# One tile later: weight splits, x tiles and gates of a projection kernel in float16 pairs, and the order of its first loads

## What is computed

```
xn   = rmsnorm(x, norm_gain)
proj = xn @ w_in                       # 1024 x (9*512 + 8)
gb, gc, hc, zc, q, k, v, o, zm, ig, fg = split(proj)
yc, conv_new = short_conv(gc * hc, conv_buf, conv_w)     # 3 taps
y_conv = gb * yc * silu(zc)
# mLSTM, 4 heads of 128, in chunks of 128 tokens, with running maxima
lf = log_sigmoid(fg + b_fgate); igh = ig + b_igate; b = cumsum(lf)
d  = exp(log_d - m_t); s = (q k^T) * d
h  = (s v + inter * q c_prev) / max(|den|, exp(-m_t))
c, n, m = new states, per chunk and per sample
y_m = rmsnorm(h) * mh_norm_gain * sigmoid(o) * silu(zm)
out = [y_conv, y_m] @ w_out ;  y = rmsnorm(x + out, final_norm_gain)
```

## Time and profile before

| what | us |
|---|---|
| median of three runs | 1125.42 (1124.85 to 1126.02) |
| the profiled execution | 1124.19 |
| its span, first to last instruction | 1122.4 |
| TensorE busy with matmuls | 1068.5 |
| vector engine busy | 538.1 |
| scalar engine busy | 340.3 |
| GpSimd busy | 256.6 |
| mean granted TensorE clock, of full speed | 0.987 |

### The profile page before, as it was taken

The page is one execution under the profiler, slowest core; times in us unless marked ns, Lnnn a source line. Parts: engine busy times, 40 slices in busy tenths (PEclk is TensorE's granted clock), DMA queues, the critical chain, the costliest instruction groups (busy, mean ns, idle before and its releaser), DMA issues. The chain is left out here.

```text
span 1122.4 us, 17994 instructions
## 1 busy us (share of the span) xinstructions
PE 1068.5 (95%) x7186; PEld 603.8 (54%) x7186; DVE 538.1 (48%) x1005; ACT 340.3 (30%) x672; POOL 256.6 (23%) x333
## 2 busy tenths in 40 slices
PE   2899999999999999899999997999999999999996
PEld 2555546565666555456665554566656555444442
DVE  4786664566443434574534344744333323333333
ACT  6546434243303242234122322422212221211111
POOL 6102303021201322111122231111111111442422
PEclk9899999999999999899999998999999999999998
DMA  9574532043200311442003115300212053255652
GB/s 223 161 154 88 133 80 48 24 123 99 69 26 12 94 44 57 136 118 69 20 18 90 48 57 147 107 32 19 93 38 90 20 197 114 97 199 203 236 211 81
DMA packets 124183, 108.73 MB, mean 97 GB/s; under 512 B 42384, under 2 KB 109092, under 8 KB 124100
## 3 DMA queue, kind: packets, MB, share of 16 engines
q1 hardware_dynamic: 84160, 66.78, 20.9%
q0 software_dynamic: 7600, 25.03, 6.1%
q10 hardware_dynamic: 32340, 15.78, 5.4%
HBM read 65.43 MB, written 33.41 MB: 88 GB/s over the span
## 5 line engine op out<-in xcount | busy, mean ns | idle before, releaser
L805 PE MATMUL bank<-xTh,Wh 128*128 128x512 f16 (+2 forms) x1304 | 422.7, 343 | 6.5 <-DMA xTl<-to 3.5
L806 PE MATMUL bank<-xTl,Wh 128*128 128x512 f16 (+2 forms) x1304 | 425.5, 343 | 0.0
L807 PE MATMUL bank<-xTh,Wl 128*128 128x512 f16 (+2 forms) x1304 | 424.8, 343 | 0.0
L807 PEld LDWEIGHTS bank<-xTh,Wl 128*128 128x128 f16 x1304 | 129.4, 99 | 121.7 <-issue 3.1
L805 PEld LDWEIGHTS bank<-xTh,Wh 128*128 128x128 f16 x1304 | 129.4, 99 | 115.7 <-DMA xTl<-to 3.7
L806 PEld LDWEIGHTS bank<-xTl,Wh 128*128 128x128 f16 x1304 | 129.4, 99 | 109.9 <-issue 4.2
L814 PE MATMUL bank<-Wh,xTh 128*128 128x128 f16 x544 | 92.8, 219 | 0.6 <-DVE ysum L163 0.6
L816 PE MATMUL bank<-Wh,xTl 128*128 128x128 f16 x544 | 92.8, 219 | 0.0
L815 PE MATMUL bank<-Wl,xTh 128*128 128x128 f16 x544 | 92.8, 219 | 0.0
L163 ACT ACTIVATE tz<-bank 128x512 f32<-128x512 f32 x32 | 19.1, 598 | 147.9 <-PE bank L807 147.1
L677 POOL TENSOR_TENSOR ysumst<-ysum,ysumst 128x1024 f16<-128x1024 f32 x16 | 34.8, 2178 | 106.5 <-ACT ysumst L163 106.5
(11 more groups left out here) (336 smaller groups left out, 1520.9 us busy)
## 6 DMA issues: line engine op xcount, KB each, us to landing
wst<-in_w_in ACTq DMA_DIRECT2D x27, 512.0 KB, 4.0
xs<-in_x_prompt SPq DMA_DIRECT2D x22, 512.0 KB, 4.1
y_ops<-ysumst POOLq DMA_DIRECT2D x16, 512.0 KB, 3.2
w_ops<-xs SPq DMA_DIRECT2D x16, 448.0 KB, 3.8
out<-xs POOLq DMA_DIRECT2D x11, 512.0 KB, 2.9
Wh<-y_ops SPq DMA_DIRECT2D x12, 448.0 KB, 3.6
Wl<-y_ops SPq DMA_DIRECT2D x12, 448.0 KB, 4.3
wst<-in_w_in SPq DMA_DIRECT2D x9, 512.0 KB, 4.6
```

Of the source, the lines that this page charges most:

```text
L805: mm(out, wh[:, k, :], xh, start=(k == 0), stop=False)
L806: mm(out, wh[:, k, :], xl, start=False, stop=False)
L807: last = mm(out, wl[:, k, :], xh, start=False, stop=(k == KT - 1))
```

## The change

It changes the tables, the first loads, and the place of the weight splits.

```diff
-X_SQUARE = [{Q: 6, GC: 7, HC: 8, ZC: 9, O: 10}, {K: 11, V: 12, GC: 13, HC: 14}, {K: 15, V: 16}]
-X_PARTS = [{Q: 5, GC: 6, HC: 7, GB: 8, O: 9, ZM: 10}, {V: 11, Q: 12, HC: 13, GB: 14}, {V: 15, Q: 16}]
-GATES_AT = [ZC, GC, GC]
-SCAN_AT = [O, GB, GB]
-TURN_AT = [ZM, ZC, ZC]
+X_SQUARE = [{Q: 6, GC: 7, HC: 8, ZC: 9, O: 10}, {K: 11, Q: 12, HC: 13, GB: 14}, {K: 15, V: 16}]
+X_PARTS = [{Q: 5, GC: 6, HC: 7, GB: 8, ZM: 9}, {V: 10, Q: 11, GC: 12, GB: 13, ZC: 14}, {V: 15, Q: 16}]
+GATES_AT = [ZC, HC, GC]
+SCAN_AT = [O, ZC, GB]
+TURN_AT = [ZM, O, ZC]
...
@@ SP, the start
-            turn_x(0)
-            turn_x(1)
-            load_w(sp, 0, 1)
-            turn_x(2)
-            load_w(sp, 0, 2)
-            turn_x(3)
-            load_rows(sp, states_in, 0, ...)
-            turn_x(4)
+            for unit in range(X_EARLY):
+                turn_x(unit)
...
@@ GpSimd, the start
             x_power(2)
+            x_power(3)
+            x_power(4)
             step(pool.memset(ones[:, :], 1.0))
...
-            x_power(3)
             for tile, first_of, rest, start in (...):
                 step(pool.memset(tile[:, :], rest))
                 step(pool.memset(first_of[:, :, 0], start))
-            x_power(4)
...
@@ TensorE, at_half
                 if t == V and first and b == 0:
+                    pe.wait_ge(states_in, 16 * 2)
+                    use_t1(3)
+                    nc.tensor.transpose(T1[:, 0:STATES_IN], prow[...], ident[...]).then_inc(t1_full, 1)
                     columns(1, MIX, t1(g, b, "mix cols", first))
...
@@ TensorE, first tile
                             if c == CH - 1:
-                                pe.wait_ge(states_in, 16 * 2)
-                                use_t1(2)
-                                nc.tensor.transpose(T1[:, 0:STATES_IN], prow[...], ident[...]).then_inc(t1_full, 1)
-                                gates(x_units(0), MIX, BT, 3)
+                                gates(x_units(0), MIX, BT, 2)
...
@@ scalar engine, act_block
                 if following == "weights":
-                    act.wait_ge(w_low, (g + 1) * NT - 1)
+                    act.wait_ge(w_low, (g + 1) * NT)
                     act.wait_ge(wo_low, 4 * g)
-                    load_w(act, g + 1, 0)
-                    load_w(act, g + 1, 1)
+                    for t in range(STAGES):
+                        load_w(act, g + 1, t)
...
-                    if following == "weights":
-                        act.wait_ge(tile_done, nth(g, b) * NT + (t + 1))
-                        split_w(g + 1, t)
-                        if t < NT - 2:
-                            act.wait_ge(w_low, (g + 1) * NT + t)
-                            load_w(act, g + 1, t + 2)
+                    if following == "weights" and t:
+                        act.wait_ge(tile_done, nth(g, b) * NT + t)
+                        split_w(g + 1, t - 1)
+                        if STAGES <= t + 1 < NT:
+                            act.wait_ge(w_low, (g + 1) * NT + (t - 1))
+                            load_w(act, g + 1, t + 1)
+                    if g and b == 0 and t == K:
+                        act.wait_ge(tile_done, g * NB * NT)
+                        split_w(g, ZM)
...
@@ scalar engine, the start
             x_square(3)
+            load_w(act, 0, 1)
+            x_square(4)
             x_high_part(2)
+            load_w(act, 0, 2)
+            x_high_part(3)
+            load_rows(act, states_in, 0, ...)
             split_w(0, 0)
-            x_square(4)
-            x_high_part(3)
+            x_high_part(4)
             act.wait_ge(bias_in, 16 * 3)
             gate_logits(0, MIX, 1)
-            x_high_part(4)
...
@@ vector engine, dve_block
-                    if following == "weights":
-                        if t == K:
+                    if following == "weights" and t:
+                        if t == V:
                             gain_w(g + 1, K)
-                        if t < NT - 1:
-                            gain_w(g + 1, t + 1)
-                        split_w(g + 1, t)
+                        gain_w(g + 1, t)
+                        split_w(g + 1, t - 1)
+                    if g and b == 0 and t == K:
+                        split_w(g, ZM)
...
@@ vector engine, the start
             x_low_part(2)
+            x_low_part(3)
             split_w(0, 0)
-            x_low_part(3)
-            gain_w(0, 1)
+            x_low_part(4)
             dve.wait_ge(bias_in, 16 * 3)
             gate_abs(0, MIX)
-            x_low_part(4)
+            gain_w(0, 1)
             gain_w(0, 2)
-            dve.wait_ge(t1_full, 3)
-            mark(copy(par[:, 0:STATES_IN], T1[:, 0:STATES_IN]).then_inc(t1_free, 1), t1_free, 3)
...
             split_w(0, 2)
+            dve.wait_ge(t1_full, 4)
+            mark(copy(par[:, 0:STATES_IN], T1[:, 0:STATES_IN]).then_inc(t1_free, 1), t1_free, 4)
             gate_scan(1, MIX, BT)
```

More of the change, by code:

```diff
@@ L470, in _ @@
             load_x(4)
-            turn_x(0)
-            turn_x(1)
-            load_w(sp, 0, 1)
-            turn_x(2)
-            load_w(sp, 0, 2)
-            turn_x(3)
-            load_rows(sp, states_in, 0, state_n.rearrange("b h p -> (b h) p"), state_conv.rearrange("b j (h p) -> (b j h) p", p=P))
-            turn_x(4)
+            for unit in range(X_EARLY):
+                turn_x(unit)
             next_w(3)
@@ L881, in at_half @@
                 if t == V and first and b == 0:
+                    pe.wait_ge(states_in, 16 * 2)
+                    use_t1(3)
+                    nc.tensor.transpose(T1[:, 0:STATES_IN], prow[0:STATES_IN, :], ident[0:STATES_IN, 0:STATES_IN]).then_inc(t1_full, 1)
                     columns(1, MIX, t1(g, b, "mix cols", first))
@@ L985, in pe_block @@
                             if c == CH - 1:
-                                pe.wait_ge(states_in, 16 * 2)
-                                use_t1(2)
-                                nc.tensor.transpose(T1[:, 0:STATES_IN], prow[0:STATES_IN, :], ident[0:STATES_IN, 0:STATES_IN]).then_inc(t1_full, 1)
-                                gates(x_units(0), MIX, BT, 3)
+                                gates(x_units(0), MIX, BT, 2)
                             x_turned(pe, 1 + c)
@@ L1340, in _ @@
             x_square(3)
+            load_w(act, 0, 1)
+            x_square(4)
             x_high_part(2)
+            load_w(act, 0, 2)
+            x_high_part(3)
+            load_rows(act, states_in, 0, state_n.rearrange("b h p -> (b h) p"), state_conv.rearrange("b j (h p) -> (b j h) p", p=P))
             split_w(0, 0)
-            x_square(4)
-            x_high_part(3)
+            x_high_part(4)
             act.wait_ge(bias_in, 16 * 3)
             gate_logits(0, MIX, 1)
-            x_high_part(4)
             mixed_start(0, 0, K, True)
@@ L1351, in _ @@
             split_w(0, 2)
-            gate_logits(1, BT, 3)
+            gate_logits(1, BT, 2)
             gate_logs(1, BT)
@@ L1793, in dve_block @@
                     at_end(g, b, t, first)
-                    if following == "weights":
-                        if t == K:
+                    if following == "weights" and t:
+                        if t == V:
                             gain_w(g + 1, K)
-                        if t < NT - 1:
-                            gain_w(g + 1, t + 1)
-                        split_w(g + 1, t)
+                        gain_w(g + 1, t)
+                        split_w(g + 1, t - 1)
+                    if g and b == 0 and t == K:
+                        split_w(g, ZM)
                     if (g, b) in SLAB_FIRST and t in (GB, ZM):
                         output_low(SLAB_FIRST[g, b] + (t == ZM))
-            GATE_COUNTS = [1, 3] + [t1(0, b, "gates", True) for b in range(NB - 1)]
+            GATE_COUNTS = [1, 2] + [t1(0, b, "gates", True) for b in range(NB - 1)]
             COLS_COUNTS = ([t1(0, 0, "mix cols", True)] + [t1(0, b, "cols", True) for b in range(NB - 1)] +
```

## The result

The changed kernel takes 1116.57 us (median of 4, 1115.34 to 1118.71) where the kernel before, on the same chip, takes 1125.72 (median of 4): ratio 0.9922, 95% interval 0.9904 to 0.9940. That is 9.2 us faster. Forecast were 16.6; the median is 0.07 us above the top of the range. The profiled execution is the slowest of the four, 1118.71 us; against the profiled one of before, 1124.19, it is only 5.5 faster. Further on, one of the five executions of experiment 1 (3989.05 us) and one of the fifteen of before beside it (1412.27) stand far from all others, and the ratios leave them out.

The account below looks back on a forecast made before the run. TensorE was taken as the bound, busy 1068.5 of 1122.4 us, so only its idling could shrink. Terms -16.2, -2.2 and +1.8 gave -16.6 us, from 1125.42 to 1108.8 us; range 1104.0 to 1116.5.

Parts of the forecast that it names:

- part 2: Start: weight and state loads leave SP's list, transposes finish sooner, block 0's gates start sooner; net 2.2 us won.
- part 1: Weight blocks of heads 1 and 2: weight splits one tile later remove `dp` waits and slow clock; 16.2 us won.
- part 3: Block 1 of head 0: x tiles, gates and scan move one tile later; small waits go, T1 waits; 1.8 us lost.
- rival (c): Weight blocks: the load's wait moves; a late third load returns half of 16.2 between GC and ZC: 1116.9; chance 0.11.
- about 0.5 us each, ahead of `kf`'s evacuation, which nobody needs before Q's half: Weight blocks: the scalar engine issues three loads in a row instead of two, about 0.5 us each, without delaying TensorE.
- I take it that this one keeps it: Block 1: the new 3.5 us T1 gap keeps full clock, as a 3.5 us gap at line 805 did.
- Rival (a): Block 1's gap is 4 us or more and costs the clock, 2.6 us: 1111.4; chance 0.14.
- The clock may hold there, but the chain, not TensorE, sets 56.1, so this is worth nothing: Start, behind block 0's gates: the vector engine's chain sets the time, so a held clock wins nothing.
- Rival (b): Start: moved loads slow the transposes as much as before, gaining only 0.9 us: 1110.1; chance 0.13.
- (d): Block 1: GpSimd finishes its sums so early that T1's wait is only 1 us: 1106.3; chance 0.04.
- (e): Block 1: tile 12's late load delays its square, the sums, states and T1: 1128 or more; chance 0.03.
- (f): Weight blocks: neither line 849 wait goes, because something else, such as y sums, holds `dp`: 1125; chance 0.03.

Follow-up runs that it names:

- experiment 1: Kernel before with only the later weight splits and the three weight loads issued together: 1111.88 us, ratio 0.9901.
- experiment 5: Changed kernel with the scalar engine's third weight load issued behind tile K's evacuation and the sample states behind tile V's: 1115.84 us, ratio 0.9926.
- experiment 8: Changed kernel with the edits of experiment 5, experiment 6 and experiment 7 together: 1107.54 us, ratio 0.9858.
- experiment 9: As experiment 8, but the three weight loads stay at the block's head and only the states move to the end of V: 1105.24 us, ratio 0.9836.
- experiment 11: As experiment 8, with unread 128-column products filling three TensorE waits in block 0 of head 0: 1104.31 us, ratio 0.9828.
- experiment 10: As experiment 8, with the final gain's broadcast load moved behind the loads of the third phase's operands: 1105.13 us, ratio 0.9835.
- experiment 13: Mended kernel: changed kernel with the states' place of experiment 9 and the edits of experiment 6, experiment 7, experiment 10 and experiment 11: 1103.71 us, ratio 0.9819.
- experiment 14: Kernel of experiment 13 without part 3, with the tables and GpSimd's list of before: 1106.93 us, ratio 0.9848.
- experiment 15: Kernel of experiment 13 without part 2: the start's order of before, its own waits filled with unread products: 1107.43 us, ratio 0.9854.
- experiment 6: Changed kernel with GpSimd's power of tile 12 behind the four sums of y in block 1: 1112.53 us, ratio 0.9899.
- experiment 7: Changed kernel with block 1's scan moved to tile O and its turn to ZM: 1113.82 us, ratio 0.9914.
- experiment 12: Changed kernel with 58 unread products filling TensorE's wait for T1 in block 1: 1113.92 us, ratio 0.9914.
- experiment 4: Changed kernel without part 3, with the five tables of before: 1111.98 us, ratio 0.9899.
- experiment 2: Kernel before with only the new order at the start: 1123.04 us, ratio 0.9995.
- experiment 3: Kernel before with only the changed tables, moving x tiles, gates and scan of block 1: 1128.38 us, ratio 1.0048.

## Why the prediction was wrong

**The sign was right, and in the profiles the parts' signs too** (part 2 can't be told from nothing by the times), and so were most of the waits, in place and size: gates of block 0 at 28.24 (27 to 28.5 was said), the wait at the half of V 1.76 (1.8), T1's wait 3.34 (3.5), chunk 2's 2.69 (2.2); the waits of `dp`, `ysum` and `cs` gone, the clock full in both weight blocks. What failed is what stood beside the waits. The median lacks 7.4 of the 16.6 us, the profile 10.7: 3.8 in part 1, 2.0 in part 2, 4.7 in part 3. That the median lies beside rival (c)'s 1116.9 is chance, since the wait that (c) names came at a fifth of its price (1.6 of 8.1 us).

**Part 1, 11 to 13 us instead of 16.2.** The failed step is "about 0.5 us each, ahead of `kf`'s evacuation, which nobody needs before Q's half". Both halves of it are wrong. The three loads took 3.04 us to issue (0.41, 0.66 and 1.92) and the states 3.03 and 3.75, where two loads and the states took 1.08 and 1.67 before. And TensorE needs `kf` evacuated some 6 us after K's end, not at Q's half: V's products, from 459.5 to 465.5, fill the other bank, and Q's first one goes into K's, which `kf` still held until 466.79. Two waits, 1.34 and 2.02, are the price, and experiment 5 takes them away by moving the issues and nothing else. The bound of "0 and 1 us a block" for a late vector engine was right for after (0.65 and 0.90 at the chunks), but only because `kf` waited first; without that it is 1.5 to 2.9 in head 2 (experiments 5, 8, 9 and 11), and 0.7 to 1.1 once the gain's load is moved too (10, 13, 14 and 15), a transfer that the prediction hadn't looked at.

**Part 3, 5.4 us lost instead of 1.8.** The failed step is "I take it that this one keeps it": a gap of 3.50 us in the trace of before left the clock alone, so one of 3.5 would. It did not. The step takes a limit from one execution, and that execution speaks against it: the same trace has the clock at 0.50 from 49 to 56, where TensorE had waited 1.39 us (until 47.60) and 1.58 (until 50.26). And where before kept it, at line 805, experiment 1, whose start is the same, lost it behind a shorter wait. Windows of before, then the wait and the window of experiment 1:

```profile
28.00:30.00 2.00, 0.53 (x9) 0.36 (x6) 1.19 (x5) 0.00 (x0) 1.08 (x7) 1.00 0.89 151
50.00:52.00 2.00, 1.74 (x7) 1.16 (x8) 1.76 (x4) 1.69 (x7) 0.00 (x0) 0.50 0.00 0
```

```profile
26.64 0.29 PE L805 MATMUL bank<-xTh,Wh 128*128 128x128 f16 x1 [3.11 <-DMA xTl<-to]
...
28.00:30.00 2.00, 1.56 (x15) 1.35 (x14) 0.29 (x2) 0.00 (x0) 1.06 (x7) 0.50 0.89 155
```

So the 3.50 that kept the clock was luck of that execution. Rival (a), at a chance of 0.14, had the outcome but not its condition, a gap of 4 us or more, and the outcome came twice: 3.1 us of slow clock behind T1's wait and 1.7 behind chunk 2's, which no rival had. The waits themselves add up to what was forecast. By the timeline:

- won before the exponentials: 1.64 (1.3 was said)
- T1's wait: 3.50 lost (3.5)
- gates without a wait: 1.27 won (1.3)
- chunk 1 and 2: 1.91 less 0.77, 1.1 lost (0.9)
- slow clock: 3.1 and 1.7, 4.8 lost (0)

The sum without the last line is 1.7, against the forecast's 1.8. Experiment 6 takes T1's wait away and wins 6.4, the wait and its clock together; the wait for `cn` at chunk 2 stays, 2.70, with its slow clock. Experiment 7 takes chunk 2's and wins 3.5 in the profile; experiment 12 keeps T1's wait and takes only the clock's part, 3.3. The clock's part is that of these profiles: behind the same T1's wait it was 1.7 in experiments 5 and 7.

**Part 2, 0.5 us instead of 2.2.** The gates came 2.27 us sooner, as reckoned (2.5), and the column products at Q's half only 0.16. "The clock may hold there, but the chain, not TensorE, sets 56.1, so this is worth nothing" is the failed step: the clock does count there. In after it fell at 29, under the gates themselves, and at 50; in experiments 4, 5, 7, 8 and 10 at 40 and again at 54, behind waits of 1.8 us for `par` and 2.1 for `sel`. All these end block 0 only 0.2 to 0.5 us sooner than before. Experiments 2, 6, 9 and 12 have the same start, their clock falls once, near 48 or 49, and they end block 0 1.5 to 1.9 us sooner. So the chain's gain is there, and whether an execution keeps it goes with where its clock falls. With the waits filled (11 and 13) it is 1.3 to 1.4.

Rival (b) fell. In after's start the scalar engine issues the two weight loads at 12.00 and 14.46 and they land 4.6 and 5.0 us later, so they run beside the first of the six transposes, issued at 15.62 and 16.94. Of the six one takes 2.03 us to issue, the others 1.23 to 1.34, where tile 3's took 2.46:

```profile
16.94 2.03 SPq L459 DMA_TRANSPOSE xTl<-yc  x1
19.08 1.24 SPq L457 DMA_TRANSPOSE xTh<-tz  x1
20.36 1.33 SPq L459 DMA_TRANSPOSE xTl<-to  x1
```

The Trainium skill (DMA: Bandwidth & Descriptors, Queues, rings and completion order) has each DMA engine take turns between the queue rows that have work, packet by packet. Nothing here speaks against that rule, but by it the start would have won 0.9 us, and the gates came 2.27 sooner: the share that the loads took from the transposes was small. Rival (c) named the right stretch, GC to ZC, with the wrong size: 0.65 and 0.90 instead of half of 16.2. Rivals (d), (e) and (f) didn't occur. The lower end of the range is not what its own terms give: the start at 3.2 and no loss in block 1 make 1103.4, not 1104.0.

**What stays open.** What decides whether a wait costs the clock isn't settled. Length alone does not: at line 805 a gap of 3.50 kept it (before) and gaps of 3.11 and 3.40 lost it (experiments 1 and 3), and for `kf` in head 2 a gap of 2.02 kept it (after) and one of 2.02 lost it (experiment 6, 0.50 from 683.2 to 686.6). One profile of each kernel gives no chance for it.

## What to carry to other kernels

When you reckon the price of a new wait on TensorE, add the slow clock behind it, even if a longer gap elsewhere in the trace left the clock alone: in the profile of after it cost as much again as the waits, 4.8 us beside 4.6 (3.5 and 1.1), and in other executions less. A DMA issue on a computing engine's list isn't free work: ask which evacuation (the copy of a result out of its PSUM bank) stands behind it and which bank the next tile wants. And when a part loses, look for the one thing in its lists that is in the wrong place before you take the part back: part 3 went from 5.4 us lost to 3.2 won by two small edits, the first measured in the kernel before and the second in the mended one.

## What the runs showed of the hardware

- TensorE's clock fell from 2.4 to 1.2 GHz (granted 0.50) behind idle gaps of 3.34, 2.69 and 2.1 us, and behind waits of 1.5 us at 50 (after) and 1.8 us at 40 (experiment 4), each time for some 3 to 7 us. In other executions it kept 1.00 behind 3.50 us (before, at 26.93), 2.02 (after, at 689.60) and 1.76 (after, at 40.74). Products that nobody reads, put into the gaps, kept it at 1.00 from 28 to 62 (experiments 11 and 13) and from 132 to 142 (experiment 12).
- The price of a slow stretch varies at one and the same wait: behind T1's wait of 3.3 us it was about 3.2 us in after and experiment 3, and 1.7 in experiments 5 and 7.
- DMA issues that the scalar engine makes in one go get longer: in the weight blocks of heads 1 and 2 the first took 0.4 us, the second 0.65, the third 1.7 to 2.7, whether it was a weight load or the states, and the states as the fourth 2.8 to 3.9. Issued at the end of V instead, the same states took 0.4 to 0.7 us in head 1 (experiments 5, 8 to 11 and 13 to 15) and 0.5 to 2.5 in head 2. What holds an issue up isn't shown: the share of the DMA engines was 1.00 during the issue of 1.67 us (before, at 454.65) and 1.08 during that of 3.03 (after, at 463).
- GpSimd's last sum of 128x256 took 0.72 us at 129.29 in after, where the vector engine stood idle for 8.18 us, and 1.05 before, at 125.33, where the vector engine was at work. The vector engine's operation on two 4x512 operands into `restart` took 1.10 us while GpSimd was summing (before, at 122.69) and 0.69 while it was idle (after, at 120.86).
